# A two-layer float32 block on one core: where the SBUF buffers begin, moved to multiples of 512 bytes

## The reference

```python
# layer 1
h = rms_norm(x, g_mix); proj = h @ w_in            # 1024 x 6664
merged = sum(sigmoid(a_i) * (attention_i(proj) @ w_br_i) for i in (moba, fox, mem))
x = x + merged @ w_out
h2 = rms_norm(x, g_ffn)
x = x + (silu(h2 @ w_gate) * (h2 @ w_up)) @ w_down  # 1024 x 2816, 2816 x 1024
# layer 2a: a gated recurrence (hg_w_in 1024 x 4096), layer_norm, a second feed-forward of 2816
# layer 2b: differential attention (da_w_in), layer_norm, then a mixture of experts:
#   router picks 2 of 8 experts for each token; each expert: gate, up 1024 x 3584, down 3584 x 1024
```

## The kernel before

| buffers | start, modulo 512 bytes |
|---|---|
| `ring`, `H`, `XH`, `XL`, `CT`, `PO`, `POT`, `VS`, `VT`, `BC`, `NG`, `GM`, `LAMB` | 128 |
| `SM` | 256 |
| `WHB`, `WLB`, `AR1`, `AR2`, `AR3`, `YH`, `YL`, `HID`, `UB`, `HTH`, `HTL`, `WHX`, `WLX`, `LZ`, `LT`, `EH`, `EL`, `ZH`, `ZL`, `ring4`, `CT2` | 192 |

## Time and profile before

### The profile page before, as it was taken

One profiled execution on the slowest core, in us unless ns is written; L12 is line 12 of the kernel. 1 busy time (PEld: TensorE's weight loads), 2 busy tenths in 40 slices (PEclk: granted clock), 3 DMA queues, 4 the chain that ended last, 5 costly groups with the idle time before them and its releaser, 6 DMA issues.

```text
span 1916.5 us, 22389 instructions
## 1 busy us (share of the span) xinstructions
PE 1837.1 (96%) x9160; PEld 1520.2 (79%) x9160; DVE 1476.7 (77%) x1432; ACT 1219.8 (64%) x1267; POOL 139.5 (7%) x115
## 2 busy tenths in 40 slices
PE   7999999999999999999969999999999999999997
PEld 6888878888988788888758887878888787888875
DVE  5646566454689754479769899999989999998997
ACT  6555545333664444355537788888778888877884
POOL 2501100000100130015120000000000000000000
PEclk9999999999999999999979999999999999999999
DMA  8433345545432555343538999999999999999994
GB/s 293 175 132 132 133 171 204 194 154 180 172 132 89 197 206 191 129 176 132 182 128 319 379 360 409 407 412 409 404 363 355 413 408 413 409 402 362 367 409 170
DMA packets 154782, 511.54 MB, mean 267 GB/s; under 512 B 4431, under 2 KB 8898, under 8 KB 140338
## 3 DMA queue, kind: packets, MB, share of 16 engines
q1 hardware_dynamic: 152674, 504.53, 69.3%
q0 software_dynamic: 1392, 4.53, 0.8%
q10 hardware_dynamic: 608, 0.99, 0.1%
HBM read 508.98 MB, written 1.05 MB: 266 GB/s over the span
## 4 chain that ended last, share of the span: by engine, by line
PE 70%; DVE 17%; DMA 6%; ACT 4%; issue 2%; POOL 0%; ACTq 0%; SPq 0%; DVEq 0%; POOLq 0%
PE PS L437 19%; PE PS L439 19%; PE PS L438 19%; DVE WLX L1876 6%; DMA ring<-in_moe_w_down 6%; DVE WLB L1876 6%; PE PS L895 2%; PE PS L1116 1%; PE PS L1117 1%; ACT WHX L1267 1%; ACT WHB L1267 1%; PE PS L1047 1%; PE PS L1049 1%; PE PS L591 1%; PE PS L1094 1%
## 5 line engine op out<-in xcount | busy, mean ns | idle before, releaser
L1267 ACT ACTIVATE WHB<-ring 128x2048 fp32r<-128x2048 f32 (+1 forms) x344 | 532.8, 1561 | 304.4 <-PE PS L439 269.7
L1876 DVE TENSOR_TENSOR WLB<-ring,WHB 128x2048 fp32r<-128x2048 f32 (+1 forms) x344 | 637.3, 1869 | 114.1 <-ACT WHB L1267 113.6
L1876 DVE TENSOR_TENSOR WLX<-ring,WHX 128x2048 fp32r<-128x2048 f32 (+1 forms) x216 | 469.6, 2195 | 53.9 <-ACT WHX L1267 53.7
L1267 ACT ACTIVATE WHX<-ring 128x2048 fp32r<-128x2048 f32 (+1 forms) x216 | 393.3, 1837 | 160.5 <-PE PS L439 122.7
L437 PE MATMUL PS<-WHB,XH 128*128 128x512 f32 (+1 forms) x640 | 256.5, 401 | 8.5 <-DVE WLB L1876 2.5
L439 PE MATMUL PS<-WHB,XL 128*128 128x512 f32 (+1 forms) x640 | 249.8, 390 | 0.0
L438 PE MATMUL PS<-WLB,XH 128*128 128x512 f32 (+1 forms) x640 | 248.6, 388 | 0.0
L437 PEld LDWEIGHTS PS<-WHB,XH 128*128 128x128 f32 x640 | 121.5, 190 | 37.0 <-issue 6.2
L439 PEld LDWEIGHTS PS<-WHB,XL 128*128 128x128 f32 x640 | 121.4, 190 | 25.8
L2770 POOL TENSOR_TENSOR SM<-SM,MH 128x8 f32<-128x8 f32 (+3 forms) x28 | 38.1, 1367 | 1409.2 <-DVE SM L1889 1409.2
L438 PEld LDWEIGHTS PS<-WLB,XH 128*128 128x128 f32 x640 | 121.4, 190 | 23.0
(11 more groups left out here) (418 smaller groups left out, 3409.6 us busy)
## 6 DMA issues: line engine op xcount, KB each, us to landing
ring<-in_moe_w_gate SPq DMA_DIRECT2D x56, 2048.0 KB, 11.1
ring<-in_moe_w_up SPq DMA_DIRECT2D x56, 2048.0 KB, 11.3
ring<-in_moe_w_down SPq DMA_DIRECT2D x56, 2048.0 KB, 11.9
ring<-in_w_in SPq DMA_DIRECT2D x13, 2048.0 KB, 8.0
ring<-in_hg_w_in SPq DMA_DIRECT2D x8, 2048.0 KB, 8.5
ring<-in_da_w_in SPq DMA_DIRECT2D x6, 2048.0 KB, 8.3
ring<-in_w_gate SPq DMA_DIRECT2D x5, 2048.0 KB, 7.8
ring<-in_w_up SPq DMA_DIRECT2D x5, 2048.0 KB, 7.8
```

Of the source, the lines that this page charges most:

```text
L1267: e.activation(hi, src, ACT.Copy).then_inc(s_hi, 1)
L1876: e.tensor_tensor(lo, src, hi.bitcast(F32), ALU.subtract).then_inc(s_lo, 1)
```

## The change

A buffer `FRONT` of 384 bytes a partition is put ahead of `ring`; nothing reads or writes it. `SM` becomes 64 bytes shorter; the columns handed out of it fit in both sizes. With that `ring` starts at byte 16896 (33 x 512), `SM` at remainder 128, and `WHB0` at byte 114176 (223 x 512). Every buffer that the table lists at 128 or at 192 starts at a multiple of 512 bytes, `SM` aside; the first group moves up by 384 bytes and the second by 320, so that from `XH` to `WHB0` it is 39,936 bytes where it was 40,000. Each engine has the same instructions in the same order with the same waits, and the DMAs are the same; only addresses differ.

```diff
+        FRONT = sb("FRONT", [128, 96])
         ring = sb("ring", [128, NSLOT, 4096])
         H = sb("H", [128, 2, D])
         XH = sb("XH", [128, 8, S], FR)
...
         MH = sb("MH", [128, 8])
-        SM = sb("SM", [128, 1008])
+        SM = sb("SM", [128, 992])
         WHB = [sb(f"WHB{i}", [128, 2048], FR) for i in range(2)]
...
         def sm(n):
             sm_at[0] += n
-            assert sm_at[0] <= 1008
+            assert sm_at[0] <= 992
             return SM[:, sm_at[0] - n:sm_at[0]]
```

## The result

| | before | changed |
|---|---|---|
| median, us | 1918.57 (4 runs) | 1906.08 (4 runs) |
| lowest to highest | 1915.44 to 1919.85 | 1905.0 to 1907.42 |
| ratio | | 0.9936, 95% interval 0.9922 to 0.9951 |
| span in the trace | 1916.5 | 1903.2 |
| first matmul of the experts at | 1004.3 | 1002.4 |

The direction was right; the gain was 12.5 us where 5.3 was forecast. The last three rows of the table are from one profiled execution of each kernel. The lines of `kernel.py` are 3 higher in the changed kernel (437 is now 440, 1876 is 1879).

The account below looks back on a forecast made before the run. TensorE was taken as the bound to 1020 us, the experts as mixed. Of 6.2 us (5.4 + 0.8), 5.3 plus 0.4 on the path, less 0.4 for weight parts, left 5.3: 1912.6 us, range 1909 to 1922.

Parts of the forecast that it names:

- rival 1: No effect: region or buffer itself, not the remainder, makes `XH`/`XL` matmuls slow; 1917.9 us, chance 0.25.
- rival 2: Slower: the stationary slice's own start counts, even multiples of 64 bytes being slow; 6.8 us lost, 1924.7, chance 0.12.
- TensorE is the bound up to the experts, and a remainder shows there.: Split-product lines hold 73.9% of the chain to 1020 us; `XH` stationary takes 229.0 ns, quick pairs 226.8.
- Equal remainders are quick.: `XH`/`XL` stationary matmuls drop to quick spacing at (0, 0): 5.4 us for 512 columns, 0.8 us for 256.
- "value 0" for (128, 192): 256-column matmuls with `XH` moving and `WHB` stationary keep their 113.4 ns spacing: no gain or loss.
- DVE and ACT: value 0, bound 0.9 us.: Pieces reading the ring in the experts keep their durations; at most 0.9 us for DVE, 0.4 for ACT.
- DMA: value 0, bound 1.8 us.: Loads' writes into SBUF unchanged; the 1.6% reading-side difference on 12.7% of 896 us bounds it at 1.8 us.
- The rule that I set aside.: Descriptors off 256-byte multiples: up to 8 extra beats per 2 KB, 12%, 14 us on chain loads; reads didn't bear it out.
- The two read ports.: Skill's independent moving and weight ports would mean zero gain; 229.0 beside 227.1 ns was held against it for `XH`.
- A quicker DMA alone: Loads alone getting quicker, worth 1.8 us, counted within rival 3's chance of 0.05.
- rival 3: More gain: remainder 0 also brings matmuls to a column a cycle, 213.3 ns; 47 us, about 1871, chance 0.05.

Follow-up runs that it names:

- all at 128, 160, 192, 256: Four kernels: the kernel before with all large buffers, load targets too, at that one remainder; 1916.02, 1915.37, 1916.85 and 1907.11 us in that order.
- only targets: Kernel before with only the load targets `ring` and `ring4` at multiples of 512, all else at its old remainder: 1908.49 us against 1919.23, ratio 0.9941.
- `ring` alone: Kernel before with only `ring` at a multiple of 512, `ring4` left at 192: 1908.4 us against 1918.03, ratio 0.9950.
- `ring4` alone: Kernel before with only `ring4` at a multiple of 512, `ring` left at 128: 1916.65 us against 1918.47, ratio 0.9993.
- the run with the operands alone: Kernel before with all buffers except `ring` (128) and `ring4` (192) at multiples of 512: 1915.77 us against 1919.23, ratio 0.9986.

## Why a saving of 2.6% a byte was worth 10 us

By the chain 12.7% of the experts, 114 us, were loads; 2.6% of that is 3 us. The slices with a DMA share of 1.0 are another measure: 11 of them in the kernel before, 527 us, 2.6% of which is 13.7. To tell these apart without addresses, the last 1/32 of every row is not loaded in the experts, from their fifth load on:

```diff
                 src = source(i)
-                e.dma_start(slot(i)[:, 0:t * n].rearrange("p (t n) -> p t n", t=src.shape[1]), src).then_inc(s_ring[SLOT[i]], 16)
+                dst = slot(i)[:, 0:t * n].rearrange("p (t n) -> p t n", t=src.shape[1])
+                if i >= N_PRE + 4:
+                    w = src.shape[2] - src.shape[2] // 32
+                    src, dst = src[:, :, 0:w], dst[:, :, 0:w]
+                e.dma_start(dst, src).then_inc(s_ring[SLOT[i]], 16)
```

> The kernel before with the last 1/32 of every row of the expert loads left out (from the fifth load on; the stale values of earlier loads are used in their place): 3.1% fewer bytes, the same number of packets, DVE, ACT and TensorE do all their work. The alignment took about 12 us of packet time off each DMA engine in the experts, 1.5 to 2.5%. Theory A, the loads set the pace wherever the DMA share is at 1.0 (11 of the 19 slices of the stage, some 530 us): a cut of 3.1% gives 10 to 16 us, 1903 to 1908. Rival B, they set it only where the chain of waits names them (12.7% of 896 us, 114 us): 3 to 4 us, 1914 to 1916.

> The same cut of 1/32 in the changed kernel, with the same part left out. Theory A: packets are already shorter; DVE's low parts are the next bound (95% busy in these slices), so the cut gives less than in the kernel before, 3 to 8 us, 1898 to 1903. Rival B: 3 to 4 us, 1902 to 1903, the same as its gain in the kernel before. The difference between the two cuts tells.

Measured (6 runs each): on the kernel before 1906.73 against 1918.59, ratio 0.9928 (0.9911 to 0.9945), 11.9 us, as theory A has it and three times what rival B has. On the changed kernel 1904.13 against 1918.59, ratio 0.9919 (0.9906 to 0.9933), 2 us under the changed kernel's 1906.1 to 1906.3 of other sets; that is less than the 3 to 8 I gave. The experts, 1200:1300 and 1500:1600 (us, then busy of TensorE, weight loads, DVE, ACT, POOL, then clock, DMA share, GB/s): before, changed, cut of before, cut of changed.

```profile
1200.00:1300.00 100.00, 95.53 (x463) 76.13 (x462) 96.34 (x63) 84.91 (x69) 0.00 (x0) 0.98 1.02 410
1500.00:1600.00 100.00, 95.13 (x457) 75.41 (x455) 95.06 (x63) 84.91 (x71) 0.00 (x0) 0.98 1.02 411
```
```profile
1200.00:1300.00 100.00, 96.59 (x471) 77.25 (x470) 98.08 (x63) 87.59 (x72) 0.00 (x0) 1.00 1.02 421
1500.00:1600.00 100.00, 96.31 (x470) 76.90 (x468) 97.63 (x64) 86.38 (x71) 0.00 (x0) 1.00 1.02 422
```
```profile
1200.00:1300.00 100.00, 96.56 (x477) 77.55 (x476) 98.02 (x65) 86.67 (x70) 0.00 (x0) 1.00 1.02 410
1500.00:1600.00 100.00, 96.55 (x480) 77.73 (x479) 98.39 (x63) 87.66 (x71) 0.00 (x0) 1.00 1.02 410
```
```profile
1200.00:1300.00 100.00, 96.54 (x471) 77.26 (x470) 98.32 (x61) 87.09 (x73) 0.00 (x0) 1.00 1.02 412
1500.00:1600.00 100.00, 96.54 (x465) 77.29 (x464) 96.80 (x63) 84.95 (x71) 0.00 (x0) 0.98 1.01 404
```

DVE is busy 96 and 95% before, 98% in the changed kernel and 98% with the cut: in these stretches DVE was 4 to 5% from being the bound itself. Loads and DVE were nearly level there, and the chain, which names one releaser at each step, put most of that time on DVE; the cut shows that it came at the pace of the loads.

That the same cut gives the changed kernel only 2 us would fit DVE as the next bound, but it doesn't show it, for the queue stayed all but full too. There it moved 41.10 MB at 101.6% and 40.29 MB at 100.8%, 39.5 and 40.0 us a MB where the uncut loads took 38.8, so a load shortened by 3% took the queue only 0 to 1% less time. In the kernel before, the cut left the time a MB as it was (39.8 us), so there it saved the queue the whole 3%.

The clock has a part in this as well. It is 0.98 in both stretches before and 1.00 in both with the changed or the cut kernel: before, at 1212 to 1216 us, it is 0.63 of full speed, after TensorE had been busy for 5.8 of 7 us. Another execution of the changed kernel (again, below) has 0.98 in 1200:1300, and its experts took 904.4 us for 900.8. So some of the experts' 11 us can have come by fewer stays at 1.2 GHz behind a shorter wait; no run parts that from the loads.

## TensorE: the distance of the two operands

> Targets of the loads and weight tiles at multiples of 512, but H, XH, XL and POT at 64. The distance of the operands is turned round: XH now starts 64 bytes behind the weight tiles modulo 512, where before it was 64 ahead. If a distance of 64 slows 512-column matmuls in either direction, XH stretches go to 229 ns (5 us more); if only the other direction does, they stay at 227. The 256-column ones: with XH stationary 113 and with XH moving 118 if the quick pair of before (moving 64 ahead of stationary) carries over by distance; 120 for both if not. By the first, with 227 kept, 2 us less than the changed kernel, 1904; with 229, 1909.

> Loads' targets at multiples of 256 (ring 256, ring4 0), XH and POT at 256, weight tiles at 0. If the distance matters only modulo 256, as the loads' targets do, it is the changed kernel again: 227 and 120 ns, 1906. If it matters modulo 512, XH stretches go to 229 or beyond: 1911 or more.

> Loads' targets and weight tiles at multiples of 256, but H, XH, XL and POT at 384, so 128 from the weight tiles modulo 256. Distances so far, XH stationary with 512 columns and the two 256-column kinds: 0 gives 227, 120, 120; +64 gives 233, 119, 113.5; -64 gives 229, 118, 113.5. If any distance other than 0 is bad for 512 columns, 128 gives 229 to 233 and 1909 to 1914 in all. If 128 is as far apart as two streams can be and clashes least, 227 with 118 and 113.5: 384 x 6.6 + 192 x 2 ns = 2.9 us less than the changed kernel, 1903.

```diff
+        FRONT = sb("FRONT", [128, 96])
         ring = sb("ring", [128, NSLOT, 4096])
+        MID = sb("MID", [128, 16])
...
-        SM = sb("SM", [128, 1008])
+        SM = sb("SM", [128, 976])
```

That is the first of the three; the second, with `XH` at 256 and the weights at 0, has `FRONT` 32, no `MID` and `SM` 1056; the third, with `XH` at 384, `FRONT` 32, `MID` 32 and `SM` 1024. Distance is the start of `XH` less that of the weight tile, modulo 256. The spacings are medians of the distances from start to start, in ns:

| distance | kernels | `XH` stationary, 512 | stationary, 256 | moving, 256 | us, ratio |
|---|---|---|---|---|---|
| 0 | changed, all at 128, 160, 192, 256, `XH` at 256 | 227 | 120 | 120 | |
| 64 | xh64 | 233 | 118 | 113.5 | 1917.11, 0.9992 (0.9983 to 1.0001) |
| 128 | xh128 | 232 | 119.5 | 119 | 1915.78, 0.9985 (0.9976 to 0.9994) |
| -64 | before, only targets, `ring` alone, `ring4` alone | 229 | 118 | 113.5 | |
| 0 modulo 256, 256 modulo 512 | xh256 | 227 | 120 | 120 | 1907.74, 0.9939 (0.9925 to 0.9953) |

The stretches behind the rows for 64 and 128 (recurrence, `XH` stationary with 512 and with 256 columns):

```profile
496.60:540.19 43.59, 43.59 (x384) 1.00 0.52 183
791.17:807.74 16.57, 16.57 (x72) 1.00 0.46 170
822.28:830.84 8.56, 8.56 (x75) 1.00 0.69 244
```
```profile
496.71:542.36 45.65, 45.64 (x384) 1.00 0.52 183
791.24:807.74 16.50, 16.50 (x72) 1.00 0.46 164
822.31:830.94 8.63, 8.63 (x75) 1.00 0.66 242
```

16.57 / 71 = 233.4 ns and 16.50 / 71 = 232.4. Neither tile's own remainder decides, since 0, 128, 160, 192 and 256 are alike at distance 0, and the region of SBUF doesn't either. That was rival 1's ground, and rival 2's. For 512 columns distance 0 is the best of the four, for 256 columns the worst.

The times of xh64 and xh128 hide a second price. Their loads go to multiples of 256, 97% of the 4096-byte packets are at 159 ns, and their experts took 902.3 and 902.2 us, as quick as in the changed kernel. But the first expert matmul starts at 1009.8 and 1010.3 us, in the changed kernel at 1002.4: 7 to 8 us are lost before the experts, where the `XH` stretches set the pace. So a distance of 64 or 128 takes back most of what the loads gain.

**Both distances in one kernel.** The recurrence's `XH` and `XL` are a view that starts 64 bytes lower, and the last, 256-column weight pieces of the feed-forwards lie 64 bytes further on in their tiles:

```diff
+        FRONT = sb("FRONT", [128, 32])
...
-        XH = sb("XH", [128, 8, S], FR)
-        XL = sb("XL", [128, 8, S], FR)
+        XHT = sb("XHT", [128, 2112], FR)
+        XLT = sb("XLT", [128, 2112], FR)
+        XH, XL = (x[:, 64:2112].rearrange("p (t n) -> p t n", t=8) for x in (XHT, XLT))
+        XHG, XLG = (x[:, 48:2096].rearrange("p (t n) -> p t n", t=8) for x in (XHT, XLT))
...
-                        place, spots = (m % 4, 0), (2 * (m % 4), 2 * (m % 4) + 1)
+                        place, spots = (m % 4, 16 if item[4] == 256 else 0), (2 * (m % 4), 2 * (m % 4) + 1)
```

> All targets of loads at multiples of 256; XH and the weight tiles at a distance of 0 modulo 256 for the 512-column matmuls, and at 64 in two places where there are 256 columns: the recurrence's XH and XL start 64 bytes lower, and the feed-forwards' last weight pieces 64 bytes further on in their tile. Expected by the spacings measured: recurrence 384 x 6.6 ns = 2.5 us less, its other 192 matmuls 2.2 ns more each, 0.4 us; last chunks 192 x 2 = 0.4 us less. Sum 2.5 us under the changed kernel, 1903.5 to 1904. If the time up to the first expert matmul shrinks by that and the end does not, the experts took it back.

Measured: 1905.25 us (6 runs), before 1918.59, ratio 0.9925 (0.9911 to 0.9940). The recurrence ran at 118.0 ns, not 113.5. So did the kernel before with its expert loads cut, whose addresses there are those of the kernel before. Three more runs on one chip:

> The kernel with the 64-byte distance in the recurrence again, beside the changed kernel. In the first run its recurrence projection ran at 118.0 ns, and so did the kernel with the addresses of before in that same set, where five kernels at this distance had 113.5 in other sets. If a stretch falls into one of two steady patterns from one execution or chip to another, this one can show 113.5 again, with 1903.5 to 1904; if something in this kernel gives 118, it does again, with 1905 to 1905.5.

> The changed kernel on the same chip as the run above, for their comparison: 1905 to 1907, the recurrence projection at 120.15 ns as in all kernels at distance 0.

> The kernel before, one look: the spacing of the recurrence projection, 113.4 to 113.6 as in its first trace or 118.0 as in the kernel with the same addresses and shorter loads. 118.0 would show that the spacing at distance 64 is not a property of the addresses alone. All else as before, 1915 to 1921.

The same kernel again (best3): 1903.51 us, ratio 0.9915 (0.9902 to 0.9929); the changed kernel beside it 1906.32, ratio 0.9937 (0.9923 to 0.9951); before 1918.77. The recurrence, in the kernel with both distances, in the kernel before (one execution, 1922.4 us), and in the cut kernel before of the earlier set:

```profile
493.32:538.62 45.30, 45.29 (x384) 1.00 0.52 184
```
```profile
492.99:536.61 43.62, 43.61 (x384) 1.00 0.51 183
```
```profile
492.88:538.18 45.30, 45.30 (x384) 1.00 0.52 184
```

Over 384 matmuls that is 118, 113.5 and 118 ns. The first two ran on one chip in one set, so it isn't the chip alone; the last two have the same addresses in that stage, so it isn't the addresses alone. One and the same spacing held from the first to the last of the 384 matmuls each time. What chooses between the two patterns stays open. The version with both distances has the lower median in both sets, by about 1 us across sets and 2.8 us on one chip, but its interval and the changed kernel's overlap: not shown to be faster.

**The changed kernel once more**, in the third set:

> The changed kernel once more, beside the others of this set on one chip: 1905 to 1907.5, a ratio of 0.9925 to 0.995.

1906.23 us, before 1918.47, ratio 0.9935 (0.9922 to 0.9948).

## The prediction, step by step

- *TensorE is the bound up to the experts, and a remainder shows there.* Right. `XH` stretches went from 229.0 to 226.6 ns where 226.8 was forecast, and the sum for them was 2448 x 2.2 ns = 5.4 us.
- *Equal remainders are quick.* Right for 512 columns: (0, 0), (128, 128), (160, 160) and (192, 192) all give 227. Wrong for 256 columns, where I took 117.7 down to 113.4 and left the recurrence at 113.4: "value 0" for (128, 192). I had no equal pair with 256 columns to read and carried the 512-column rule over. The two kinds went to 120: 384 x 6.6 = 2.5 us and 192 x 2.2 = 0.4 us lost, in place of 0.8 gained. The forecast of 5.3 us for TensorE becomes some 5.4 - 2.9 = 2.5; the run with the operands alone gave 3.5, interval 0.8 to 4.4.
- *DVE and ACT: value 0, bound 0.9 us.* Right within the bound. DVE's 4 ns on 336 pieces would be 1.3 us, but a second execution of the kernel before had 2282 too.
- *DMA: value 0, bound 1.8 us.* This is the step that failed. It measured 9.6 to 10.7 us. Two things in it were wrong. The bound of 1.6% came from the reading side, where rows off a multiple of 256 bytes in HBM cost nothing that I could see; it was carried over to the writing side, which moved by 2.6%. And it was multiplied by the 12.7% that the chain puts on loads, where the slices with a full queue, 527 us, were the better stretch: 2.6% of those is 13.7 us, and the packets' own times give 12. Some 10 of it came through. That DVE, nearly level, held back the rest is likely and not shown.
- *The rule that I set aside.* The Trainium skill (DMA: Bandwidth & Descriptors, How a descriptor splits into AXI transactions) says that a transaction must start at a multiple of 256 bytes, so that a descriptor off such a multiple costs more beats of 32 bytes. The prediction's estimate from it, up to 8 beats more on 2 KB, 12% and 14 us, was worked out too high: counted as the Trainium skill counts, a start of 128 costs 4 beats more whatever the length. As an estimate that is 6% for 2 KB, 3% for 4 KB, 1.6% for 8 KB, and 2.9% for the mix of packets between 1500 and 1600 us. The runs agree on the 256: targets at 0 and 256 are quick, at 128, 160 and 192 slow. They agree on the amount for 128 as well: the time a MB is 2.7% higher, by 4.5 to 5.6 ns a packet. Four beats are 128 bytes, and those take 4.7 ns by the packets' own times ((309 - 159) ns for 4096 bytes more). They don't agree in two things: 192 costs no more than 128, where the same count gives 6 beats, and a quarter of the loads off the multiple cost next to nothing. So the rule should have been priced in, and the reading side of rows 9, whose targets in SBUF were all off the multiple, was no ground to set it aside.
- *The two read ports.* The Trainium skill (SBUF — State Buffer, Who interferes with whom) calls TensorE's two SBUF read ports independent. The spacings don't bear out that the place of one operand to the other costs nothing: moving one by 64 bytes against the other changes the spacing by 2 to 7 ns.
- *Rivals.* Rivals 1 and 2 are refuted. "A quicker DMA alone" was hidden in rival 3 with a chance of 0.05 and 1.8 us; it should have been a rival of its own, priced at 2 to 3% of the 527 us with a full queue.

## What to carry to other kernels

Let the SBUF targets of large loads start at multiples of 256 bytes where a stage's DMA queue is full: it was worth 0.5% here for a filler. Look at the distance between TensorE's operands in the same step, since 64 or 128 bytes between them cost 7 to 8 us here. Price a saving per byte by the stretches in which the DMA share is 1.0 and the next engine's busy share, not by the share of the chain of waits, which hides a queue that runs level with an engine. A row that shows no effect on the reading side bounds nothing on the writing side, and a spacing read at one width is not the spacing at another.

## What the runs showed of the hardware

- Loads into SBUF at a start of 0 or 256 modulo 512: 38.8 us of engine time a MB in a full queue (1500 to 1600 us) and 97% of the experts' 4096-byte packets at 159 ns. At 128, 160 or 192: 39.8 to 39.9 us and 46 to 54%. Within a full queue the difference is 4.5 to 5.6 ns a packet for 2048, 4096 and 8192 bytes alike.
- The spacing of back-to-back matmuls with 128 x 128 stationary fp32r operands depends on the distance of the two operands' starts modulo 256: 512 columns take 227 ns at distance 0, 229 at -64, 232 at 128 and 233 at 64; 256 columns take 120 at 0 in both roles; with the weight tile moving 118 at 64 and -64 and 119.5 at 128, with the weight tile stationary 113.5 at 64, 113.5 or 118 at -64 and 119 at 128.
- At -64 with the weight tile stationary, the same addresses gave 113.5 ns in the kernel before and 118.0 in the one with its expert loads cut, each steady over 384 matmuls.
